# Another bank pair for one query product, the output gate read by ScalarE, and thin products spread out among wide ones

## The chip, the cores and the metric

One NeuronCore of a Trainium2 chip runs the whole program. The metric is device time in microseconds (us); smaller is better. Engines are named as in the profile: PE (TensorE matmuls), PEld (its weight loads), DVE (VectorE), ACT (ScalarE), POOL (GpSimd), SP (SyncE, which here issues the weight DMAs). PSUM has eight banks of 512 float32 columns, numbered 0 to 7; they matter for this change.

## The reference

Two transformer blocks over 256 tokens of width 1024, in float32. The first block mixes a stick-breaking attention and an RWKV-7 time mix; the second has a dilated attention with a short convolution, a cross attention to a memory, and an MLP. What the change touches:

```
# RWKV-7 branch, first block
g  = sigmoid(xg) @ g_up                              # the output gate
kk = (k * k_k) per head
kk = kk / max(norm(kk, per head), 1e-12)             # 8 heads of 64
...
y  = group_norm(wkv7_scan(...)) * lnx_w + lnx_b
bonus = sum(r * k * r_k, per head) * v
out = (y + bonus) * g

# second block
proj = rms_norm(x) @ w_in_2 ; q, k, v, ... = split(proj)
```

The norm per head needs a sum over the 64 features of each head. Features lie on partitions, so the kernel makes the sum with a product by a 0/1 matrix `gather` that gives 8 rows (one per head), and copies the 8 inverses back to all features by a product with a 0/1 matrix `spread` whose contraction has 8 rows. These are the products of few columns and of few rows.

## The kernel before, in words

Every weight matrix is cut into units of 128x2048 elements (1 MB). SP loads a unit into `raw`; ACT rounds it to `whi` (L1271), DVE takes the rest `wlo = raw - whi` (L1762, called `lo`), and PE multiplies with both. There are three buffers of each, so unit u+3 is rounded when PE has used unit u. All engines run programs of their own, in a fixed order written out by hand, and wait for each other by semaphores. Nothing reorders the work.

Activations are held as `xh` and `xl` (together `xhl`). `by_feature` multiplies one unit with 48 matmuls of 256 columns. `by_feature_wide` does it with 16 matmuls of 512 columns (`whi` against both halves) and 16 of 256 (`wlo`), in two output tiles f = 0 and 1, one per bank of a pair. ACT copies the second halves out of the banks (`second_halves`), and then DVE adds the first halves (`summed`). A bank pair is free again when `summed` has been signalled.

First block, where the change touches it:

- The loop over `U_RW` (7 units, in banks 0, 1, 3). After the fifth unit (i = 4) PE makes the four `gather` products (two instructions each) into bank 4. ACT takes the square root after it has seen the end of the sixth unit (i = 5, `krs`), and DVE in its own step i = 5 clamps it and takes the reciprocal (L1850, L1851), which signals `kk_rs`. After that DVE changes the keys (L1855, L1856) and goes on with step 6.
- The loop over `U_QK` (4 wide units, bank pairs (6,7) and (0,1) in turn). After the first one PE waits for `kk_rs` and makes the four `spread` products into banks 4 and 5. Before the second one it waits for `out_evac` 7, DVE's read of the last `U_RW` unit (L1823).
- The value units `U_V` (two). Between them PE makes the gate product into banks 4 and 5 (`gup`) and the bonus product into banks 6 and 7 (`rkk`), and signals `bonus_mm`. DVE then reads the gate twice: times `lnx_w` into `rw[:, 0:4]` (L1897), and, after the bonus (L1899), as the factor of `rw[:, 4:8]` (L1903), which signals `gn_pre`.
- PE waits for `gn_pre` before it overwrites banks 4 and 5 with the first attention logits (`sk`, `sq`), and then runs eight gate units.

Second block, at its start: `keys_around("n3", U_KM[1])` multiplies a unit of the memory keys into banks 0 and 1 and turns the rows of x in banks 2 to 5. Then come the four query and key units `U_QK2`: the first by `by_feature` into bank 6, followed by a small product that copies the norm's row (`dg`, `one`) into bank 4, the second (wide) into banks 0 and 1, the third into 6 and 7, the fourth into 0 and 1. Because banks 0 and 1 still hold the memory keys, the second waits for `summed` of `km`, which DVE makes in `key_sum(1)` behind a `lo`.

Of the kernel before, what the change touches and what calls it, by code (L numbers as in the profile page):

```python
# [6 lines left out]
P = 128  # L7
SEQ = 256
# [4 lines left out]
NPAIR = HW // P  # L13
HD = 64
NH = HW // HD
# [71 lines left out]
def block_kernel(nc, A, out, dbg=None):  # L87
# [9 lines left out]
    with ctx:  # L97
# [5 lines left out]
        def sem(name):  # L103
            if name not in sems:
                sems[name] = ctx.enter_context(nc.semaphore(name))
            return sems[name]
# [142 lines left out]
        def bank(b):  # L249
            return PS[:, b * 512:(b + 1) * 512]  # L250
# [4 lines left out]
        def halved(kind, n):  # L255
            return sum(HALVED[o] for o in list(HALVED)[:list(HALVED).index(kind)]) + n
# [6 lines left out]
        def C(name):  # L263
            a, b = CCOL[name]
            return cst[:, a:b]
# [5 lines left out]
        def par_col(name, i=0):  # L271
            c = PCOL[name] + i
            return par[:, c:c + 1]
# [76 lines left out]
        VM_BANKS = (0, 1, 4, 5)  # L350
        MLP_BANKS = ((2, 3), (0, 1))
        QK_BANKS = ((6, 7), (0, 1))
        QK2_BANKS = (None, (0, 1), (6, 7), (0, 1))
        KM_BANKS = (0, 1)
        RW_BANK = [(0, 1, 3)[i % 3] for i in range(len(U_RW))]

# [84 lines left out]
        def _(pe):  # L441
            def mm(o, l, r, start, stop, **kw):
                return nc.tensor.matmul(o, l, r, start=start, stop=stop, **kw)  # L443
# [75 lines left out]
            def by_feature_wide(u, both, banks, later=0, before=None, between=None, amidst=None, first=None):  # L519


                n = units[u][1]
                wh, wl = split(u, n, later)
                for f in range(2):
                    if before:
                        before(f)
                    fs = slice(f * P, (f + 1) * P)
                    o = bank(banks[f])
                    for k in range(KD):
                        if amidst:  # L530
                            amidst(f, k)
                        mm(o, wh[:, k, fs], both[:, k].rearrange("p a t -> p (a t)"), k == 0, False, skip_group_check=True)
                    for k in range(KD):
                        last = mm(o[:, 0:SEQ], wl[:, k, fs], both[:, k, 0], False, k == KD - 1, skip_group_check=True)
                    if f == 0:
                        if first:
                            last.then_inc(sem(first), 1)
                        if between:
                            between()
                last.then_inc(sem("units_used"), 1)  # L540

            def by_token(u, hi, lo, k0, b, first, end, later=0, between=None):

                n = units[u][1]
                kt = UNIT // n
                wh, wl = split(u, n, later)
                nc_ = n // 512
                if end:
                    steps = [(k, t, c) for t in range(NT) for c in range(nc_) for k in range(kt)]
                else:  # L550
                    steps = [(k, t, c) for k in range(kt) for t in range(NT) for c in range(nc_)]
                for k, t, c in steps:
                    ts = slice(t * P, (t + 1) * P)
                    o = bank(b[t * nc_ + c] if isinstance(b, tuple) else b + t * nc_ + c)
                    ns = slice(c * 512, (c + 1) * 512)
                    mm(o, hi[:, k0 + k, ts], wh[:, k, ns], first and k == 0, False)
                    mm(o, hi[:, k0 + k, ts], wl[:, k, ns], False, False)
                    last = mm(o, lo[:, k0 + k, ts], wh[:, k, ns], False, end and k == kt - 1)
                    if end and k == kt - 1 and (t, c) != (NT - 1, nc_ - 1):
                        last.then_inc(sem("part_done"), 1)  # L560
                        if between:
                            between(t, c)
                last.then_inc(sem("units_used"), 1)
# [88 lines left out]
            def amid_first(i):  # L652
                if i == 0:
                    return lambda part: first_rows(1) if part == 1 else None
                if i == 2:
                    return lambda f: scale_row("n1", 2)
                if i == 3:
                    return lambda f: lora_products()

            for i, u in enumerate(U_RW):  # L660
                if i >= 3:
                    pe.wait_ge(sem("out_evac"), i - 2)
                by_feature(u, xh, xl, RW_BANK[i], None if i else "n1", amid_first(i))
                if i == 4:

                    pe.wait_ge(sem("kk_sq"), 1)
                    pe.wait_ge(sem("lora_evac"), 1)
                    pe.wait_ge(sem("cst_loaded"), 16)
                    for j in range(NPAIR):
                        last = mm(PS[0:NH, 4 * 512:4 * 512 + SEQ], C("gather")[:, NH * j:NH * (j + 1)], kq[:, j, :], j == 0,  # L670
                                  j == NPAIR - 1)
                    last.then_inc(sem("kk_ss"), 1)

            for i, u in enumerate(U_QK):
                if i == 1:
                    pe.wait_ge(sem("out_evac"), 7)
                elif i >= 2:
                    pe.wait_ge(sem("summed"), halved("qk", i - 1))
                by_feature_wide(u, xhl, QK_BANKS[i % 2])
                if i == 0:  # L680

                    pe.wait_ge(sem("kk_rs"), 1)
                    for j in range(NPAIR):
                        last = mm(PS[:, 4 * 512 + j * SEQ:4 * 512 + (j + 1) * SEQ], C("spread")[0:NH, j * P:(j + 1) * P], krs[:],
                                  True, True)
                    last.then_inc(sem("kk_spread"), 1)
            for i, u in enumerate(U_V):
                by_token(u, xh, xl, 4 * i, 2, i == 0, i == 1)
                if i == 0:
# [159 lines left out]
                    pairs(kk, eP, "pair_mm", 4)  # L849

            pe.wait_ge(sem("gn_pre"), 1)
            def gate_unit(i):

                before(i)
                if i == 0:
                    pe.wait_ge(sem("summed"), halved("qk", 4))
                else:
                    pe.wait_ge(sem("summed"), halved("gate", i))
                by_feature_wide(U_G[i], xhl, (0, 1), between=lambda: amid(i))
                behind(i)  # L860
# [206 lines left out]
            for i, u in enumerate(U_QK2):  # L1067
                if i == 0:
                    by_feature(u, xh, xl, 6, "n3")
                    scale_row("n3", 4)  # L1070
                    continue
                if i == 1:
                    pe.wait_ge(sem("summed"), halved("km", 2))
                elif i == 2:
                    pe.wait_ge(sem("out2_evac"), 1)
                else:
                    pe.wait_ge(sem("summed"), halved("qk2", 1))
                by_feature_wide(u, xhl, QK2_BANKS[i])
            by_token(U_V2[0], xh, xl, 0, 2, True, False)

            def dilated_logits(p_):
# [185 lines left out]
        def _(act):  # L1267
# [14 lines left out]
            def hi(u, n=0, step=0):  # L1282

                if u >= NU:
                    return
                act.wait_ge(raw_loaded[u % RING], 16 * (u // RING + 1) + 16 * (step // RING) * n)
                if u >= RING:
                    act.wait_ge(sem("units_used"), u - RING + 1 + step * n)
                A_(whi[u % RING][:], raw[u % RING][:], ACT.Copy).then_inc(sem("hi_done"), 1)

            def after(u):

                hi(u + RING)
                act.wait_ge(sem("units_used"), u + 1)
# [100 lines left out]
            for i, u in enumerate(U_QK):  # L1395
                act.wait_ge(sem("units_used"), u + 1)
                second_halves((sq, sk)[i // 2][:, 2 * (i % 2):2 * (i % 2) + 2, :], QK_BANKS[i % 2]).then_inc(sem("second"), 1)
                hi(u + RING)
            hi(U_V[0] + RING)
            after(U_V[1])  # L1400
            act.wait_ge(norm_sem("n1", "dg"), nth("n1", "dg", 1))
            for t in range(NT):
# [344 lines left out]
        def _(dve):  # L1747
# [144 lines left out]
            lo(U_V[0] + RING)  # L1892

            dve.wait_ge(sem("bonus_mm"), 1)
            dve.wait_ge(sem("rw_pre"), 1)
            for j in range(NPAIR):
                V.tensor_scalar(rw[:, j, :], PS[:, 4 * 512 + j * SEQ:4 * 512 + (j + 1) * SEQ], par_col("lnx_w", j), None, ALU.mult)  # L1897
            for j in range(2):
                last = V.tensor_tensor(bon[:, 2 * j:2 * j + 2, :], bank(6 + j).rearrange("p (j t) -> p j t", j=2),  # L1899
                                       rw[:, 8 + 2 * j:10 + 2 * j, :], ALU.mult)  # L1900
            link(last)
            for j in range(NPAIR):
                last = V.scalar_tensor_tensor(out=rw[:, 4 + j, :], in0=bon[:, j, :], scalar=par_col("lnx_b", j),  # L1903
                                              in1=PS[:, 4 * 512 + j * SEQ:4 * 512 + (j + 1) * SEQ], op0=ALU.add, op1=ALU.mult)
            last.then_inc(sem("gn_pre"), 1)
            lo(U_V[1] + RING)
            def pair_out(dst, mask, n_, b=2):

# [510 lines left out]
```

## Time and profile before

| | |
|---|---|
| median of 3 runs | 841.4 us (840.96 to 841.78) |
| profiled execution | 841.16 us, of which the profile's span is 839.4 us |
| PE busy | 824.6 us, 98% |
| DVE busy | 586.9 us, 70% |
| ACT busy | 430.8 us, 51% |
| mean granted clock of TensorE | 0.997 of full speed |

The span is cut by the profile into what each engine did; 1.8 us of the execution's time lie outside it. The time of a row is the start in us from the start of the span, then the duration; an idle time in square brackets is what lay ahead of it on that engine, and who ended it.

### The profile page before, as it was taken

To read this page: it belongs to the slowest core of one execution; us is meant where nothing else is said; L and a number is where in the kernel's file an instruction comes from. 1 tells how busy PE (TensorE), PEld (TensorE's weight loads), DVE (VectorE), ACT (ScalarE), POOL (GpSimd) and SP (SyncE) were. 2 spreads that over 40 slices of the span, in tenths; PEclk is the share of its full clock that TensorE was granted. 3 is DMA by queue.
4 is the path that set the end of the run, shared out by engine and by line. 5 is a ranking of instruction groups with operands and counts; after the bars stand their busy time and mean duration, and the time that the engine had idled before them with its cause. 6 is when DMAs were issued, how large, how long until landed. Compare 5 with 4: busy or idle time off the path is not lost.

```text
span 839.4 us, 14921 instructions
## 1 busy us (share of the span) xinstructions
PE 824.6 (98%) x6332; PEld 715.2 (85%) x6332; DVE 586.9 (70%) x693; ACT 430.8 (51%) x529; POOL 6.4 (1%) x8
## 2 busy tenths in 40 slices
PE   9999999999999999999998999999999999999997
PEld 9998788888989888888887888888888888888885
DVE  5999865656887666656678567795764866676664
ACT  6644344474387544544466365546654544444443
POOL 0000010000000000000000000000000000000000
PEclk9999999999999999999999999999999999999999
DMA  9845513331764555565545553546423365555541
GB/s 301 289 152 177 175 53 102 103 102 52 280 209 159 180 201 185 165 216 185 200 157 177 168 194 108 192 143 201 167 100 126 133 228 182 180 180 183 192 149 50
DMA packets 96999, 140.55 MB, mean 167 GB/s; under 512 B 2480, under 2 KB 79408, under 8 KB 96944
## 3 DMA queue, kind: packets, MB, share of 16 engines
q1 hardware_dynamic: 96512, 139.36, 49.7%
q8 instruction: 43, 0.70, 0.3%
q10 hardware_dynamic: 432, 0.39, 0.2%
q14 instruction: 12, 0.10, 0.0%
HBM read 138.69 MB, written 1.05 MB: 166 GB/s over the span
## 4 chain that ended last, share of the span: by engine, by line
PE 83%; DVE 10%; ACT 3%; issue 3%; DMA 1%; POOL 0%; ACTq 0%; DVEq 0%; POOLq 0%
PE PS L443 81%; DVE wlo L1762 3%; ACT whi L1271 1%; PE PS L569 1%; DMA raw<-in_w_in_dram 1%; ACT st L1271 1%; DVE rw L1828 1%; ACT xhl L1271 1%; DVE diff L1825 1%; DVE stg L1823 1%; PE PS L1100 0%; DVE cs L1845 0%; PE PS L716 0%; DVE xhl L1789 0%; DVE TT L1924 0%
## 5 line engine op out<-in xcount | busy, mean ns | idle before, releaser
L1762 DVE TENSOR_TENSOR wlo<-raw,whi 128x2048 fp32r<-128x2048 f32 x122 | 278.2, 2289 | 78.7 <-ACT whi L1271 78.5
L443 PE MATMUL PS<-xhl,whi 128*128 128x512 f32 (+1 forms) x1328 | 308.5, 365 | 3.9 <-DVE km L1767 2.9
L1271 ACT ACTIVATE whi<-raw 128x2048 fp32r<-128x2048 f32 (+1 forms) x130 | 241.3, 1859 | 93.6 <-PE PS L443 90.1
L443 PEld LDWEIGHTS PS<-xhl,whi 128*128 128x128 f32 x1328 | 230.3, 190 | 40.3 <-DVE km L1767 3.1
L443 PE MATMUL PS<-xhl,wlo 128*128 128x256 f32 x1136 | 180.3, 282 | 0.1
L443 PEld LDWEIGHTS PS<-xhl,wlo 128*128 128x128 f32 x1136 | 163.7, 191 | 9.7 <-DVE wlo L1803 0.3
L443 PE MATMUL PS<-whi,fh 128*128 128x512 f32 x216 | 84.3, 391 | 0.0
L443 PE MATMUL PS<-wlo,fh 128*128 128x512 f32 x216 | 84.3, 390 | 0.0
L443 PE MATMUL PS<-whi,fl 128*128 128x512 f32 x216 | 84.0, 389 | 0.0
L1767 DVE TENSOR_TENSOR fa<-PS,fa 128x512 f32<-128x512 f32 x25 | 17.3, 691 | 62.7 <-ACT fa L1271 62.7
L443 PEld LDWEIGHTS PS<-whi,fl 128*128 128x128 f32 x216 | 40.6, 188 | 8.6
L443 PEld LDWEIGHTS PS<-whi,fh 128*128 128x128 f32 x216 | 40.7, 188 | 7.8
L443 PEld LDWEIGHTS PS<-wlo,fh 128*128 128x128 f32 x216 | 40.7, 188 | 7.5
L1271 ACT ACTIVATE fa<-PS 128x512 f32<-128x512 f32 x25 | 14.7, 589 | 52.4 <-PE PS L443 52.4
L1789 DVE SCALAR_TENSOR_TENSOR xhl<-PS,par,xhl 128x256 fp32r<-128x256 f32 x40 | 16.7, 476 | 11.7 <-ACT xhl L1271 11.7
L1271 ACT ACTIVATE fh<-fa 128x512 fp32r<-128x512 f32 x16 | 10.1, 633 | 25.9 <-DVE fa L2357 25.9
L1271 ACT ACTIVATE xhl<-PS,par 128x256 fp32r<-128x256 f32 x40 | 15.7, 481 | 12.1 <-PE PS L569 12.1
L443 PE MATMUL PS<-whi,memhl 128*128 128x512 f32 x64 | 20.7, 397 | 0.1
L443 PE MATMUL PS<-whi,xhl 128*128 128x512 f32 x64 | 20.7, 394 | 0.0
L1271 ACT ACTIVATE fh<-fb 128x512 fp32r<-128x512 f32 x11 | 7.0, 632 | 24.9 <-DVE fb L2173 24.9
L1271 ACT ACTIVATE gates<-PS 128x512 f32<-128x512 f32 x8 | 4.8, 597 | 27.9 <-PE PS L443 27.9
L1271 ACT ACTIVATE junk<-xres 128x1024 f32<-128x1024 f32 (+1 forms) x14 | 13.2, 945 | 9.9 <-DVE xres L2116 8.7
(327 smaller groups left out, 1035.3 us busy)
## 6 DMA issues: line engine op xcount, KB each, us to landing
raw<-in_w_in_dram SPq DMA_DIRECT2D x32, 1024.0 KB, 5.3
raw<-in_w_up_dram SPq DMA_DIRECT2D x16, 1024.0 KB, 5.3
raw<-in_w_down_dram SPq DMA_DIRECT2D x16, 1024.0 KB, 5.1
raw<-in_w_ffn_gate_dram SPq DMA_DIRECT2D x11, 1024.0 KB, 5.3
raw<-in_w_ffn_up_dram SPq DMA_DIRECT2D x11, 1024.0 KB, 5.3
raw<-in_w_ffn_down_dram SPq DMA_DIRECT2D x11, 1024.0 KB, 5.6
raw<-in_w_kv_mem_dram SPq DMA_DIRECT2D x8, 1024.0 KB, 5.3
raw<-in_w_o_dram SPq DMA_DIRECT2D x4, 1024.0 KB, 8.2
```

The costliest lines, as they stand in the source:

```text
L443: return nc.tensor.matmul(o, l, r, start=start, stop=stop, **kw)
L569: last = nc.tensor.transpose(PS[:, o:o + P], src[:, t, f * P:(f + 1) * P], C("ident"))
L1271: return nc.scalar.activation(o, i, f, **kw)
L1762: V.tensor_tensor(wlo[u % RING][:], raw[u % RING][:], whi[u % RING][:].bitcast(f32), ALU.subtract) \
L1767: return V.tensor_tensor(dst, tiles(banks)[:, :, 0], dst, ALU.add)
L1789: V.scalar_tensor_tensor(out=lo_[:, f0 + f, :], in0=PS[:, b * 512 + c * SEQ:b * 512 + (c + 1) * SEQ], scalar=par_col(g, f), in1=hi_[:, f0 ...
L1823: V.tensor_tensor(s[:, :, 1:SEQ + 1], two(RW_BANK[i]), spread(rs1[:]), ALU.mult).then_inc(sem("out_evac"), 1)
L1825: link(V.tensor_tensor(diff[:], s[:, :, 0:SEQ], s[:, :, 1:SEQ + 1], ALU.subtract))
L1828: last = V.scalar_tensor_tensor(out=rw[:, r, :], in0=diff[:, f, :], scalar=par_col("mu_rw", r), in1=s[:, f, 1:SEQ + 1], op0=ALU.mult, op1= ...
```

## The change

Three edits, each with its semaphores:

1. The second query unit of the second block goes to banks 2 and 3 instead of 0 and 1. The wait for `summed` of `km` moves to the fourth unit, which still uses banks 0 and 1. The first value unit, which uses banks 2 and 3, gets a wait for the second unit's sum.
2. ACT reads the output gate from PSUM: times `lnx_w` into `rw[:, 0:4]`, and as it is into `rw[:, 4:8]`, then signals `g_read`. DVE reads only the bonus from PSUM, signals `gn_pre` right behind that, and makes the last product out of SBUF. PE waits for both.
3. The four `gather` products no longer stand in one row after the fifth unit: they stand in the sixth unit's first tile, ahead of k = 0, 2, 4 and 6. The four `spread` products no longer stand after the first wide unit: they stand inside it, ahead of k = 2 and k = 6 of each of its two tiles. The wait for `kk_rs` goes with the first of them.

```diff
-        QK2_BANKS = (None, (0, 1), (6, 7), (0, 1))
+        QK2_BANKS = (None, (2, 3), (6, 7), (0, 1))
@@ PE
+            def gather_squares(f, k):
+                if f or k % 2:
+                    return
+                j = k // 2
+                if j == 0:
+                    pe.wait_ge(sem("kk_sq"), 1)
+                    pe.wait_ge(sem("lora_evac"), 1)
+                    pe.wait_ge(sem("cst_loaded"), 16)
+                last = mm(PS[0:NH, 4 * 512:4 * 512 + SEQ], C("gather")[:, NH * j:NH * (j + 1)], kq[:, j, :], j == 0, j == NPAIR - 1)
+                if j == NPAIR - 1:
+                    last.then_inc(sem("kk_ss"), 1)
+            def spread_norms(f, k):
+                if k not in (2, 6):
+                    return
+                j = 2 * f + k // 4
+                if j == 0:
+                    pe.wait_ge(sem("kk_rs"), 1)
+                last = mm(PS[:, 4 * 512 + j * SEQ:4 * 512 + (j + 1) * SEQ], C("spread")[0:NH, j * P:(j + 1) * P], krs[:], True, True)
+                if j == NPAIR - 1:
+                    last.then_inc(sem("kk_spread"), 1)
             for i, u in enumerate(U_RW):
                 ...
-                by_feature(u, xh, xl, RW_BANK[i], None if i else "n1", amid_first(i))
-                if i == 4:
-                    (the four gather products, with the same waits)
+                by_feature(u, xh, xl, RW_BANK[i], None if i else "n1", amid_first(i), 0, gather_squares if i == 5 else None)
             for i, u in enumerate(U_QK):
                 ...
-                by_feature_wide(u, xhl, QK_BANKS[i % 2])
-                if i == 0:
-                    pe.wait_ge(sem("kk_rs"), 1)
-                    (the four spread products)
+                by_feature_wide(u, xhl, QK_BANKS[i % 2], amidst=None if i else spread_norms)
...
             pe.wait_ge(sem("gn_pre"), 1)
+            pe.wait_ge(sem("g_read"), 1)
...
-                if i == 1:
+                if i == 2:
+                    pe.wait_ge(sem("out2_evac"), 1)
+                elif i == 3:
                     pe.wait_ge(sem("summed"), halved("km", 2))
-                elif i == 2:
-                    pe.wait_ge(sem("out2_evac"), 1)
-                else:
-                    pe.wait_ge(sem("summed"), halved("qk2", 1))
                 by_feature_wide(u, xhl, QK2_BANKS[i])
+            pe.wait_ge(sem("summed"), halved("qk2", 1))
             by_token(U_V2[0], xh, xl, 0, 2, True, False)
@@ ACT, between hi(U_V[0] + RING) and after(U_V[1])
+            act.wait_ge(sem("bonus_mm"), 1)
+            act.wait_ge(sem("rw_pre"), 1)
+            for j in range(NPAIR):
+                A_(rw[:, j, :], PS[:, 4 * 512 + j * SEQ:4 * 512 + (j + 1) * SEQ], ACT.Copy, scale=par_col("lnx_w", j))
+            for j in range(2):
+                last = A_(rw[:, 4 + 2 * j:6 + 2 * j, :], bank(4 + j).rearrange("p (j t) -> p j t", j=2), ACT.Copy)
+            last.then_inc(sem("g_read"), 1)
@@ DVE
-            dve.wait_ge(sem("rw_pre"), 1)
-            for j in range(NPAIR):
-                V.tensor_scalar(rw[:, j, :], PS[...], par_col("lnx_w", j), None, ALU.mult)
             for j in range(2):
                 last = V.tensor_tensor(bon[...], bank(6 + j)..., rw[...], ALU.mult)
-            link(last)
+            last.then_inc(sem("gn_pre"), 1)
+            dve.wait_ge(sem("gn_pre"), 1)
+            dve.wait_ge(sem("g_read"), 1)
             for j in range(NPAIR):
-                last = V.scalar_tensor_tensor(out=rw[:, 4 + j, :], ..., in1=PS[...], op0=ALU.add, op1=ALU.mult)
-            last.then_inc(sem("gn_pre"), 1)
+                last = V.scalar_tensor_tensor(out=rw[:, 4 + j, :], ..., in1=rw[:, 4 + j, :], op0=ALU.add, op1=ALU.mult)
+            link(last)
```

## Rows read from the trace of the kernel before

**Rows 1.** Page, part 1: engine, busy us, share of span, instructions.
```profile
PE 824.6 (98%) x6332; PEld 715.2 (85%) x6332; DVE 586.9 (70%) x693; ACT 430.8 (51%) x529; POOL 6.4 (1%) x8
```

**Rows 2.** Waits of PE: released by, total us, times, longest us.
```profile
PE PS L443 <- DVE km L1767: 2.9, 1, 2.9
PE PS L443 <- DVE rw L1903: 1.8, 1, 1.8
```

**Rows 3.** Stretches: length; busy us of PE, PEld, DVE, ACT, POOL; PEclk; DMA.
```profile
30.00:60.00 30.00, 30.00 (x223) 27.38 (x220) 29.38 (x44) 13.53 (x15) 0.00 (x0) 1.00 0.66 217
60.00:94.50 34.50, 32.54 (x165) 27.18 (x163) 34.07 (x40) 16.03 (x13) 0.00 (x0) 1.00 0.56 176
```

**Rows 4.** PE in order of time at the start of the second block.
```profile
455.09 0.71 PE L443 MATMUL PS<-dg,one 128*128 128x128 f32 x4
458.74 3.63 PE L443 MATMUL PS<-xhl,whi 128*128 128x512 f32 x8 [2.94 <-DVE km L1767]
462.21 1.11 PE L443 MATMUL PS<-xhl,wlo 128*128 128x256 f32 x8
```

**Rows 5.** The same view as group 3, of two stretches there.
```profile
455.60:458.70 3.10, 0.20 (x2) 0.01 (x1) 2.90 (x3) 2.35 (x3) 0.00 (x0) 0.99 0.95 322
458.70:462.10 3.40, 3.36 (x8) 2.69 (x9) 2.78 (x2) 0.00 (x0) 0.00 (x0) 0.51 0.85 263
```

**Rows 6.** DVE in order of time, same place.
```profile
452.15 2.29 DVE L1762 TENSOR_TENSOR wlo<-raw,whi 128x2048 fp32r<-128x2048 f32 x1 [0.76 <-ACT whi L1271]
...
455.80 2.29 DVE L1762 TENSOR_TENSOR wlo<-raw,whi 128x2048 fp32r<-128x2048 f32 x1 [0.76 <-ACT whi L1271]
458.01 0.68 DVE L1767 TENSOR_TENSOR km<-PS,km 128x512 f32<-128x512 f32 x1
458.61 0.68 DVE L2199 TENSOR_TENSOR q<-PS,rs 128x512 f32<-128x512 f32 x1
```

**Rows 7.** PE in order of time around the gather products.
```profile
39.56 0.28 PE L443 MATMUL PS<-xhl,wlo 128*128 128x256 f32 x1
39.77 1.89 PE L443 MATMUL PS<-kq,cst 128*8 128x256 f32 x8
...
41.93 0.28 PE L443 MATMUL PS<-xhl,wlo 128*128 128x256 f32 x1
```

**Rows 8.** PE in order of time, first two wide units and the spread products.
```profile
53.21 2.00 PE L443 MATMUL PS<-xhl,whi 128*128 128x512 f32 x8
...
57.84 1.11 PE L443 MATMUL PS<-xhl,wlo 128*128 128x256 f32 x8
58.89 1.99 PE L443 MATMUL PS<-krs,cst 8*128 8x256 f32 x8
60.91 2.11 PE L443 MATMUL PS<-xhl,whi 128*128 128x512 f32 x8
62.87 1.11 PE L443 MATMUL PS<-xhl,wlo 128*128 128x256 f32 x8
...
66.94 0.50 PE L443 MATMUL PS<-xhl,whi 128*128 128x512 f32 x1 [0.17 <-DVE sq L1767]
```

**Rows 9.** DVE in order of time, steps 5 and 6 of its loop.
```profile
55.72 1.74 DVE L1851 RECIPROCAL krs<-krs 8x256 f32<-8x256 f32 x1
...
60.18 0.68 DVE L1823 TENSOR_TENSOR stg<-PS,rs 128x512 f32<-128x512 f32 x1
```

**Rows 10.** PE in order of time, end of the value units.
```profile
92.36 0.39 PE L443 MATMUL PS<-whi,xhl 128*128 128x512 f32 x1
94.50 0.92 PE L443 MATMUL PS<-sq,sk 64*128 64x256 f32 x8 [1.75 <-DVE rw L1903]
```

**Rows 11.** DVE in order of time, same place.
```profile
91.48 1.28 DVE L1899 TENSOR_TENSOR bon<-PS,rw 128x512 f32<-128x512 f32 x2
92.79 1.66 DVE L1903 SCALAR_TENSOR_TENSOR rw<-bon,par,PS 128x256 f32<-128x256 f32 x4
```

**Rows 12.** ACT in order of time: four reads of PSUM with a bias, and a wait.
```profile
36.02 1.55 ACT L1271 ACTIVATE sg<-PS,par 128x256 f32<-128x256 f32 x4
...
92.85 1.91 ACT L1271 ACTIVATE whi<-raw 128x2048 fp32r<-128x2048 f32 x1 [7.00 <-PE PS L443]
```

More of the change, by code:

```diff
@@ L662, in _ @@
                     pe.wait_ge(sem("out_evac"), i - 2)
-                by_feature(u, xh, xl, RW_BANK[i], None if i else "n1", amid_first(i))
-                if i == 4:
-                    pe.wait_ge(sem("kk_sq"), 1)
-                    pe.wait_ge(sem("lora_evac"), 1)
-                    pe.wait_ge(sem("cst_loaded"), 16)
-                    for j in range(NPAIR):
-                        last = mm(PS[0:NH, 4 * 512:4 * 512 + SEQ], C("gather")[:, NH * j:NH * (j + 1)], kq[:, j, :], j == 0,
-                                  j == NPAIR - 1)
-                    last.then_inc(sem("kk_ss"), 1)
+                by_feature(u, xh, xl, RW_BANK[i], None if i else "n1", amid_first(i), 0, gather_squares if i == 5 else None)
             for i, u in enumerate(U_QK):
@@ L678, in _ @@
                     pe.wait_ge(sem("summed"), halved("qk", i - 1))
-                by_feature_wide(u, xhl, QK_BANKS[i % 2])
-                if i == 0:
-                    pe.wait_ge(sem("kk_rs"), 1)
[L683 to L686, printed above, removed]
+                by_feature_wide(u, xhl, QK_BANKS[i % 2], amidst=None if i else spread_norms)
             for i, u in enumerate(U_V):
@@ L1894, in _ @@
             dve.wait_ge(sem("bonus_mm"), 1)
-            dve.wait_ge(sem("rw_pre"), 1)
-            for j in range(NPAIR):
-                V.tensor_scalar(rw[:, j, :], PS[:, 4 * 512 + j * SEQ:4 * 512 + (j + 1) * SEQ], par_col("lnx_w", j), None, ALU.mult)
             for j in range(2):
@@ L1900, in _ @@
                                        rw[:, 8 + 2 * j:10 + 2 * j, :], ALU.mult)
-            link(last)
+            last.then_inc(sem("gn_pre"), 1)
+            dve.wait_ge(sem("gn_pre"), 1)
+            dve.wait_ge(sem("g_read"), 1)
             for j in range(NPAIR):
                 last = V.scalar_tensor_tensor(out=rw[:, 4 + j, :], in0=bon[:, j, :], scalar=par_col("lnx_b", j),
-                                              in1=PS[:, 4 * 512 + j * SEQ:4 * 512 + (j + 1) * SEQ], op0=ALU.add, op1=ALU.mult)
-            last.then_inc(sem("gn_pre"), 1)
+                                              in1=rw[:, 4 + j, :], op0=ALU.add, op1=ALU.mult)
+            link(last)
             lo(U_V[1] + RING)
```

## The prediction

> **What bounds the kernel now.** I read the page's busy shares first: PE is busy for 98% of the span [rows 1], so only its pauses and its clock can give anything back. The table of waits of PE names two pauses worth having, 2.9 us ended by DVE's sum of the memory keys and 1.8 us ended by DVE's last use of the gate [rows 2]. Each is one that the change takes away. Third I read the busy time by stretch. From 30 to 94.5 us DVE is nearly as full as PE: 29.38 of 30 us, then 34.07 of 34.5 us [rows 3]. There DVE runs late behind PE, and a wait of PE for DVE that the change puts earlier has to be priced against DVE's own clock time. Last I read both engines in order of time at each place, and the granted clock around the long pause.
>
> **Edit 1, other banks (second block).** After the small row product at 455.09 us, whose four matmuls start 0.11 apart and whose stream is thus done at about 455.64, PE stands still until 458.74 [rows 4]. It waits for the memory-key sum, which DVE starts at 458.01, behind a 2.29 us `lo` [rows 6]. The second unit needs nothing else: its own `lo` is the one of 452.15 to 454.44 [rows 6], and banks 2 and 3 were last read for the operands that the first unit has already multiplied. So it starts at 455.64: 3.10 us earlier, and 0.11 more because a product that follows a wait starts slower (its first eight matmuls take 2.11 against 2.00 us, [rows 8]). The pause has a second price. In the stretch behind it the granted clock is 0.51 of full speed, 1.2 instead of 2.4 GHz, and back at 1.00 after that; during the pause PE did nothing [rows 5]. The eight wide matmuls took 458.74 to 462.21, 3.47 us, where the same eight after a wait take 60.91 to 62.87, 1.96 us [rows 8]: 1.51 us. With no pause there is no reason for the clock to fall. Sum: 3.10 + 0.11 + 1.51 = 4.72 us gained.
>
> Is something late next? The third unit would start at 455.64 + 5.58 = 461.2 (a wide unit is 53.21 to 57.84 plus eight matmuls of 0.12, [rows 8]). It needs the `lo` that ends at 458.09 and the first unit's read that ends at 459.29 [rows 6]. Both are done 2 us before. The fourth needs the key sum (458.69), the value unit a sum that DVE makes about 1.3 us after the second unit ends; both have a unit or two of room. From there on ACT and DVE work behind PE at the pace of its units, as before, and the gain is kept to the end. Bounds: 3.0 us if the clock falls here all the same, 4.8 at best.
>
> **Edit 2, ACT takes the gate.** PE's last value product starts at 92.36 and would let the logits start at 92.68 (0.23 for its stream, 0.09 to change to 64 rows); they start at 94.50 [rows 10], 1.82 us later. DVE did 4 multiplies by `lnx_w`, the bonus (1.28) and then 1.66 us of final products before `gn_pre` [rows 11]. Now `gn_pre` comes behind the bonus. ACT's reads: four of 128x256 take 1.55 us by the nearest row, and two of twice the width not more than 1.55 together [rows 12], so at most 3.1 us, in a hole of 7.00 us in which ACT waits for the end of the value units [rows 12]. Nothing but its own next `hi` is queued behind them. DVE's final products wait for `g_read` and so hold up the `lo` behind them, but that one waits for the `hi` after the value units anyway. Alone, this edit is worth the 1.82 us. Whether it still is depends on when PE comes here, which edit 3 decides.
>
> **Edit 3, the thin products.** First their direct price. The gather row: from the dense matmul at 39.56 to the one at 41.93 is 2.37 us, of which three dense steps are 0.36 and the eight instructions at 0.216 each 1.73 [rows 7]; 0.28 us is left for going to 8 columns and back. Four excursions instead of one: 3 x 0.28 = 0.85 us more on PE. The spread row: the dense work of the first wide unit ends at 58.79 and the next unit starts at 60.91, effectively 61.02 with its slower start; of these 2.23 us 1.73 are the products, 0.10 is the wait for L1823 (60.18 + 0.68, [rows 8, 9]), and 0.40 is the way in and out. Four excursions cost 4 x 0.40.
>
> The Trainium skill speaks against this edit. Its page TensorEngine Tiling (Array Packing), section Key Properties, says that changing the tiling mode drains the TensorE. If each thin product counts as such a change, eight excursions pay it where two did. The 0.28 and 0.40 us above are this case's numbers for it, and they are in the sum.
>
> Then the wait. The spread products need the reciprocal that DVE ends at 57.46 [rows 9]. Before, PE asked for it at 58.79, after the whole unit. Now it asks at k = 2 of the first tile. The unit starts at 53.21 + 0.85 = 54.06, two wide matmuls take 0.46, so PE is at the wait at 54.52 and stands there until about 57.50: **a new pause of 3.0 us**. Nothing makes DVE earlier: it is full up to that point [rows 3], its order is unchanged up to there, and the square root that it needs comes from ACT after the sixth unit, one unit before it is due. This pause hides the 0.85 us of the gather.
>
> From 57.50: the rest of the unit 5.58 - 0.46 = 5.12 us, the spread products 1.73, their excursions 1.60 less the 0.10 of the first way in, which the wait hides. The unit ends at 65.85. In the old kernel this point is 61.02, so PE is 4.83 us late. It wins back what it used to wait before the third unit: from 60.91 to 66.94 is 6.03 us for a unit of 5.58, 0.45 us [rows 8]. That leaves 4.38 us. From here PE is the later of the two engines: DVE's first query sum came at 66.21 and will come within half a us of that, and its queue has until 92.6 + 4.4 = 97.0 us for what it had done at 94.45. PE thus reaches the logits at 92.68 + 4.38 = 97.06 instead of 94.50: **2.56 us lost**. The gate is ready then even by the old order, give or take 0.1, so edit 2's 1.82 us are swallowed by edit 3 and not to be added.
>
> **Sum.** -4.72 + 2.56 = -2.16 us. Against the profiled execution's 841.16 us that is 839.0; this execution lies 0.24 below the median of 841.4, so I say 839.3 us. Below, 0.2% (1.7 us) is what a measurement of this kernel can tell from no change.
>
> **What isn't priced yet: the clock at the new pause.** A pause of 3.1 us halved the clock [rows 4, 5]; the one of 1.8 us did not, the clock is 1.00 over its stretch [rows 3]. The new one, 3.0 us, is nearer to the first. Bounds: 0, and 1.5 us if the loss of the old place comes again. That one case is too little to know whether 3.0 us always do it, and before and after this pause PE is at work; I give it somewhat less than even.
>
> **The rivals.**
> - *Clock halved at the new pause* (B). For: the row of the second block. It moves the 1.51 us from there to here: 839.3 + 1.5 = 840.8 us. The change then is within what can't be told from none.
> - *Clock halved, and kept low by the thin products* (C), the slower case. Behind the old pause PE ran dense 512-column products, and the clock was back after 3.4 us. Behind the new one a third of the time goes to products of 8 rows. If these don't count as work and the clock stays at half until the unit ends, the 8.3 us from 57.5 cost 1.51/1.96 = 77% more, 6.4 us: 845.7. It decides the sign from about 2.2 us on, that is if the clock stays low much longer than the 3.4 us of the old place. Against: between 30 and 60 us eight thin instructions in one row left the clock at 1.00 [rows 3, 7].
> - *No new pause* (D): the wait is met because DVE gets through earlier than its rows say. Then edit 3 costs PE 0.85 + 1.20 - 0.45 = 1.6 us, edit 2 gives back its 1.82, and the sum is -4.9: 836.5. Against: DVE has 0.6 us of idle time in the 30 us before 60, so it can't be 3 us earlier.
> - *Edit 1 doesn't do what it says* (E): the second unit starts early but the third waits in its place. Then the 4.72 shrink towards zero and edit 3's 2.56 stand alone: 844. Against: the 2 us of room above.
>
> **Chances.** Forecast (A) 0.48, own range 838.4 to 840.2; B 0.32 (840.2 to 841.6); C 0.07; D 0.06; E 0.03; the rest, 0.04, is spread. Leaving out C, most of D and E gives a range of 837.6 to 842.2. Faster by over 0.2% means under 839.7: nearly nine tenths of A, all of D and a little of B, 0.51. Slower by over 0.2% means over 843.1: C and E in the main, 0.08. Within: 0.41.
>
> **What would show it.** In the order of time, PE with an idle time of about 3 us ended by DVE's `krs` reciprocal, near 57.5, and the first wide unit ending near 65.9; the granted clock of 57 to 62 us tells A from B, and that of 62 to 66 B from C. The logits at about 97, with no wait for `rw`. The `g_read` copies on ACT in a hole of its time. Near 458 (2.6 us later than now) no wait for `km`, and a clock of 1.00. The prediction is wrong if PE meets `kk_rs` without a pause, if an excursion costs clearly more than 0.4 us, or if another unit of the second block takes over the wait.

## The result

The change made the kernel slower: 842.91 us median of 20 runs (840.62 to 847.32) against 841.29 us of the kernel before (20 runs, 839.58 to 842.99), so the medians lie 1.6 us apart; the ratio over all runs is 1.0029 with a 95% interval of 1.0017 to 1.0042. The forecast was 839.3 us, range 837.6 to 842.2. The profiled execution of the changed kernel took 845.2 us, of which 843.4 are the span. The 20 single runs lie in groups: four from 840.6 to 841.3, seven from 842.1 to 843.1, six from 845.1 to 845.4 and three above 846.5. The mean granted clock of the single runs goes down with the groups: 0.995 to 0.997, then 0.993 to 0.994, 0.990 to 0.991, and 0.988. The profile below is from the third group.

The waits of PE after the change (released by, total us, times, longest). They answer to [rows 2]: both old waits are gone, one new one is there.

```profile
PE PS L443 <- DVE krs L1866: 2.7, 1, 2.7
PE PS L443 <- POOL one L1255: 1.0, 1, 1.0
PE PS L443 <- ACT xhl L1279: 0.7, 2, 0.3
```

PE in order of time in the first wide unit. It answers to [rows 8].

```profile
54.24 0.63 PE L443 MATMUL PS<-xhl,whi 128*128 128x512 f32 x2
57.58 0.69 PE L443 MATMUL PS<-krs,cst 8*128 8x256 f32 x2 [2.71 <-DVE krs L1866]
58.20 1.22 PE L443 MATMUL PS<-xhl,whi 128*128 128x512 f32 x4
59.36 1.22 PE L443 MATMUL PS<-krs,cst 8*128 8x256 f32 x2
60.50 1.22 PE L443 MATMUL PS<-xhl,whi 128*128 128x512 f32 x2
61.52 1.91 PE L443 MATMUL PS<-xhl,wlo 128*128 128x256 f32 x8
...
71.24 2.78 PE L443 MATMUL PS<-xhl,whi 128*128 128x512 f32 x8
```

PE asks for the reciprocal after two wide matmuls and gets it at 57.58. From the second thin product on everything takes nearly twice as long: eight `wlo` matmuls take 1.91 us where they took 1.11 [rows 8]. The stretches of the same profile (length; busy us of PE, PEld, DVE, ACT, POOL; granted clock; DMA share; GB/s) say why:

```profile
54.50:57.50 3.00, 0.37 (x2) 0.00 (x0) 2.97 (x4) 2.98 (x2) 0.00 (x0) 1.00 0.24 33
57.50:59.30 1.80, 1.72 (x6) 0.96 (x6) 1.70 (x7) 0.21 (x1) 0.00 (x0) 0.99 1.01 380
59.30:72.90 13.60, 13.60 (x37) 9.38 (x37) 7.70 (x14) 4.37 (x5) 0.00 (x0) 0.50 0.28 97
72.90:78.00 5.10, 5.10 (x31) 4.51 (x30) 4.05 (x3) 1.17 (x2) 0.00 (x0) 1.00 0.11 25
```

The clock is at half (1.2 instead of 2.4 GHz) for 13.6 us, four times as long as in [rows 5], and it does not fall during the pause but 1.8 us after its end. DVE, the full engine here before [rows 3], now works for only 7.70 of 13.60 us: 5.76 us of the rest it waits for ACT's copy of a second half (`sq`, until 72.11), which follows PE's late unit.

PE at the logits, against [rows 10]: no wait, but at 103.25 instead of 94.50.

```profile
102.94 0.39 PE L443 MATMUL PS<-whi,xhl 128*128 128x512 f32 x1
103.25 0.92 PE L443 MATMUL PS<-sq,sk 64*128 64x256 f32 x8
```

ACT in the same stretch, against [rows 12]: it takes the gate in 2.54 us (97.91 to 100.45), in a hole of its time, and is done 2.8 us before PE comes for the banks at 103.25.

```profile
97.91 1.57 ACT L1279 ACTIVATE rw<-PS,par 128x256 f32<-128x256 f32 x4 [1.48 <-PE PS L443]
99.35 1.10 ACT L1279 ACTIVATE rw<-PS 128x512 f32<-128x512 f32 x2
103.42 1.91 ACT L1279 ACTIVATE whi<-raw 128x2048 fp32r<-128x2048 f32 x1 [2.97 <-PE PS L443]
```

PE at the start of the second block, against [rows 4]: the second query unit follows the row product at once, and at full speed (2.09 us for eight wide matmuls instead of 3.63).

```profile
463.87 0.71 PE L443 MATMUL PS<-dg,one 128*128 128x128 f32 x4
464.33 2.09 PE L443 MATMUL PS<-xhl,whi 128*128 128x512 f32 x8
466.27 1.11 PE L443 MATMUL PS<-xhl,wlo 128*128 128x256 f32 x8
```

So the books of this execution are: 8.75 us later at the logits (103.25 - 94.50), 4.7 us won back at 464 us, 4.0 us longer in the span (843.4 - 839.4).

### The profile page after: what moved, and what is told of

It is laid out like the page before. It is cut to its first block, busy times and chain, and to the rows that moved or that the text cites. A ratio compares the mean times of both kernels' runs of the same rounds, so it can differ in the third digit from the quotient of the medians.

```text
span 843.4 us, 14925 instructions
## 1 busy us (share of the span) xinstructions
PE 830.9 (99%) x6332; PEld 717.1 (85%) x6332; DVE 585.8 (69%) x689; ACT 433.4 (51%) x535; POOL 6.4 (1%) x8
## 4 chain that ended last, share of the span: by engine, by line
PE 91%; DVE 5%; ACT 2%; issue 2%; DMA 1%; ACTq 0%
PE PS L443 89%; DVE wlo L1777 1%; PE PS L569 1%; ACT st L1279 1%; DMA xres<-in_x_dram 1%; ACT whi L1279 1%; DVE rw L1843 0%; DVE diff L1840 0%; DVE stg L1838 0%; PE PS L1108 0%; DVE cs L1860 0%; PE PS L724 0%; DVE st L1985 0%; ACT xhl L1279 0%; DVE krs L1866 0%
## 5 line engine op out<-in xcount | busy, mean ns | idle before, releaser
L443 PE MATMUL PS<-xhl,whi 128*128 128x512 f32 (+1 forms) x1328 | 311.7, 366 | 0.8 <-ACT xhl L1279 0.7
```

## Experiments

The theory going in: edit 1 wins 4.7 us and edit 2 up to 1.8; edit 3 loses on PE's path by its pause and its excursions, and loses 1.5 us more for every 3.4 us of halved clock, which thin products behind a pause prolong. Every kernel was timed 5 to 11 times beside the kernel before, on one chip per group (one for `e1_banks` to `e12_banks_gate`, another for `p1_pause_row` to `p3_full_pieces` and `p7_full_rows`, the first again for `p8_thin_no_wait` and `p4_gather_only`). In the first group the kernel before took 841.55 us, in the second 841.57, in the third 841.39. Gains are differences of medians; the ratios are taken over all runs.

**One edit at a time.** `e1_banks` is the kernel before with edit 1:

```diff
-        QK2_BANKS = (None, (0, 1), (6, 7), (0, 1))
+        QK2_BANKS = (None, (2, 3), (6, 7), (0, 1))
   (and the waits of the change's first part)
```

> Edit 1 alone: the second query unit of the second block in banks 2 and 3. Theory: it takes away the 3.1 us pause of PE, its slow restart and the low clock behind it, so 4.7 us: about 836.6 us beside 841.3, with no wait for km in the profile, and the clock at 1.00 from 455 to 470 us. It is tied to nothing in the first block, so it gives the same in full whatever edits 2 and 3 do. Rival 1: the clock falls at some other place instead, then only the pause is won, 3.1 us: 838.2. Rival 2: another wait of the second block takes its place: over 840.

Measured: 836.74 us (836.55 to 837.22), ratio 0.9944 [0.9930, 0.9958]: 4.8 us faster. No wait for `km`; the clock is 1.00 from 455 to 470 us. Both rivals fall. Its profile also shows something that the profile of before did not: behind the unchanged row of spread products the clock is at half.

```profile
58.00:61.30 3.30, 3.30 (x18) 2.60 (x17) 3.16 (x9) 0.86 (x1) 0.00 (x0) 1.00 0.64 247
61.30:64.80 3.50, 3.50 (x11) 2.79 (x10) 3.46 (x5) 3.50 (x5) 0.00 (x0) 0.51 0.03 7
64.80:70.00 5.20, 5.20 (x31) 4.57 (x31) 5.17 (x8) 2.42 (x3) 0.00 (x0) 1.00 0.62 202
```

PE has no pause worth the name there: 3.30 of 3.30 us busy ahead of the fall, 1.99 of them in products of 8 rows. So the clock can fall behind a row of thin products with no pause, in some executions and not in others. In time it cost little here: this execution is the fastest of its five (836.55 us). The wait for `rw` is 0.6 us in it instead of the 1.8 of [rows 2], so 1.2 of the 1.5 us came out of that wait.

`e2_gate` is the kernel before with edit 2 (ACT's six reads, `gn_pre` behind the bonus, PE's wait for `g_read`).

> Edit 2 alone: ACT reads the gate. Theory: PE comes to the logits at 92.7 us instead of 94.5 and the gain is kept: 1.8 us, about 839.5 us. Rival: DVE or ACT is behind PE in the eight gate units anyway, so that PE waits there for what it won: within 0.3 us of the kernel before.

Measured: 840.22 us (839.37 to 841.77), ratio 0.9981 [0.9972, 0.9990]: 1.3 us faster. The wait for `rw` is gone and the gain is kept in the main, so the rival falls; it is 0.5 us short of the 1.8. Its profiled execution was the slowest of its eleven and has the half clock behind the spread row as well (61.4 to 64.8 us), and for 6.8 us at the old place at 457. When the clock falls at 61 us PE comes later to the value units' end and the wait for `rw` is shorter to begin with (0.6 us in `e1_banks`), so there is less to win. Without edit 2 DVE lets PE go on at 94.50 in the kernel before and at 94.59 in `e1_banks`, whenever PE comes. That this is why 0.5 us are missing from the median is likely, not shown.

`e3_thin` is the kernel before with edit 3, both `gather_squares` and `spread_norms`.

> Edit 3 alone: the thin products in pieces. Theory: a pause of 3.0 us at the reciprocal of krs, then the clock at 1.2 GHz for several stretches while thin products are mixed in; logits at 97 us plus 1.5 us for each 3.4 us of low clock. So about 4.7 us above the whole change: 847.6 us, single runs from 845 to 852. Rival: the loss of the whole change comes from edit 1 or 2, and this one is under 1 us slower than before: below 842.3.

Measured: 848.83 us (845.61 to 850.77), ratio 1.0075 [1.0053, 1.0097]: 7.3 us slower, 1.2 more than expected; what the 1.2 are stays open. The whole loss of the change, and more, is edit 3. The low stretch of its profile is the one of the whole change again:

```profile
57.50:59.60 2.10, 1.26 (x5) 0.84 (x6) 2.03 (x6) 0.96 (x1) 0.00 (x0) 1.00 0.91 288
59.60:73.30 13.70, 13.70 (x38) 9.01 (x37) 7.52 (x15) 3.72 (x5) 0.00 (x0) 0.50 0.32 107
```

`e12_banks_gate` is the change without edit 3.

> Edits 1 and 2 without edit 3. Theory: both gains stand beside each other, 4.7 + 1.8 = 6.5 us: about 834.8 us, with hardly any spread between runs, since both long pauses of PE are gone. Rival: edit 2's gain is lost in the gate units: 836.6.

Measured: 835.27 us (834.85 to 836.85), ratio 0.9928 [0.9914, 0.9942]: 6.3 us faster than before. The two gains stand beside each other. It is faster than both kernels. The "hardly any spread" is a miss: one of six runs is at 836.85. In its profile the clock is at 1.00 up to the logits, and PE comes to them without a wait at 93.28, not at 92.68; it was 0.7 us later than in the kernel before already at the spread row (59.56 against 58.89), ahead of anything that edit 2 touches.

**Pause, thin products, or both.** `p1_pause_row` is the whole change, with the pause but without thin products inside the unit:

```diff
             def spread_norms(f, k):
-                if k not in (2, 6):
-                    return
-                (one product)
+                if (f, k) == (0, 2):
+                    pe.wait_ge(sem("kk_rs"), 1)
...
                 by_feature_wide(u, xhl, QK_BANKS[i % 2], amidst=None if i else spread_norms)
+                if i == 0:
+                    (the four spread products in one row)
```

> The whole change, but the first wide unit only waits for kk_rs at k = 2 and has no thin products inside; the four spread products follow it in one row, as before. The 3 us pause stays. Theory (thin products mixed in hold the clock low behind the pause): the clock is low for one stretch of 3.4 us, at most two, and the time is 838.1 us plus 1.5 for each: 839.6 to 841. Rival (the pause alone makes a long low stretch): the clock stays low as long as in the whole change, and the time is its 842.9 less the 1.2 us of three excursions saved: 841.7 or more.

Measured: 839.81 us (838.36 to 840.04), ratio 0.9975 [0.9966, 0.9985]. Two of ten runs are at 838.4, the other eight within 0.5 us of 839.8: the sum without a low stretch, and with one. The profile has the same pause and one short low stretch:

```profile
54.50:57.50 3.00, 0.35 (x2) 0.00 (x0) 2.96 (x4) 2.98 (x2) 0.00 (x0) 1.00 0.23 28
57.50:58.50 1.00, 0.94 (x4) 0.79 (x5) 0.93 (x5) 0.19 (x1) 0.00 (x0) 1.00 0.96 356
58.50:61.90 3.40, 3.40 (x14) 3.01 (x13) 3.26 (x8) 1.49 (x2) 0.00 (x0) 0.50 0.46 179
61.90:66.00 4.10, 4.10 (x22) 3.48 (x22) 4.10 (x7) 2.91 (x4) 0.00 (x0) 1.00 0.05 8
```

So a pause of this length is mostly followed by a lower clock (eight runs of ten), and without the thin pieces behind it for 3.4 us only, by this profile and by the times. The rival, that the pause alone makes the long stretch, falls.

`p2_thin_late` is the whole change with the same four pieces in the second wide unit, where nothing has to be waited for on their account:

```diff
-                by_feature_wide(u, xhl, QK_BANKS[i % 2], amidst=None if i else spread_norms)
+                by_feature_wide(u, xhl, QK_BANKS[i % 2], amidst=spread_norms if i == 1 else None)
```

> The whole change, but the four spread products stand inside the second wide unit instead of the first, where kk_rs has long come: the same thin products among wide ones, no pause. Theory (it needs the pause): the clock stays at 1.00, PE reaches the logits at about 95.5 us, and the time is 837.6 us with little spread. Rival (thin products among wide ones lower the clock by themselves): the clock falls in the sixth RWKV unit or in this one in most runs, 839 to 843 us.

Measured: 838.48 us (837.56 to 840.61), ratio 0.9958 [0.9944, 0.9971]. Two of five runs are at the 837.6 of the theory, two near 838.5, and one, the profiled one, 3 us above. That one has the clock at half for 6.8 us from 62.5 us on, over three of the four pieces, behind the 1.0 us wait for `stg`:

```profile
62.50:69.30 6.80, 6.80 (x19) 4.46 (x19) 6.77 (x9) 3.16 (x3) 0.00 (x0) 0.50 0.48 156
```

The theory's "little spread" is a miss: with thin pieces and without the 3 us pause the clock can be low too, but no run of the five has the length of the change.

`p8_thin_no_wait` puts the four pieces closer together, in that unit's second tile, 3 us behind the wait:

```diff
-                if k not in (2, 6):
+                if f == 0 or k % 2:
                     return
-                j = 2 * f + k // 4
+                j = k // 2
```

> As p2_thin_late, but the four spread products all stand in the second tile of the second wide unit, ahead of k = 0, 2, 4 and 6, so that no wait lies near them: 2.8 us of wide products before, and thin and wide ones in close turns, 2.1 us of wide whi products to 3.3 us of thin ones and their excursions. The low stretches of p2 began at 62.5 us, behind a 1.0 us wait and the first piece. Theory (thin products count as too little work, whatever the wait): this closer mixture lowers the clock in most runs, 839 to 842 us. Rival (it takes a pause before them): the clock stays at 1.00 and all runs are near 837.6 us.

Measured: 838.23 us (837.65 to 839.54), ratio 0.9959 [0.9946, 0.9973]: between the two. PE in order of time, from its profile (839.22 us):

```profile
64.09 0.69 PE L443 MATMUL PS<-krs,cst 8*128 8x256 f32 x2
64.72 0.73 PE L443 MATMUL PS<-xhl,whi 128*128 128x512 f32 x2
65.38 0.69 PE L443 MATMUL PS<-krs,cst 8*128 8x256 f32 x2
...
67.95 0.69 PE L443 MATMUL PS<-krs,cst 8*128 8x256 f32 x2
68.58 1.12 PE L443 MATMUL PS<-xhl,whi 128*128 128x512 f32 x2
69.50 1.91 PE L443 MATMUL PS<-xhl,wlo 128*128 128x256 f32 x8
```

The first rows give the price of an excursion at full clock: a thin piece and two wide matmuls take 65.38 - 64.09 = 1.29 us, of which 0.46 is the wide ones and 0.43 the piece's stream, so 0.40 us, the figure of the prediction. The last rows take nearly twice their time: the clock falls right after the last piece, with PE busy throughout since its wait for `stg` ended at 61.10, and stays low for 3.4 us.

```profile
65.30:68.70 3.40, 3.40 (x12) 1.60 (x12) 3.37 (x6) 0.47 (x1) 0.00 (x0) 1.00 0.76 240
68.70:72.10 3.40, 3.40 (x13) 3.02 (x14) 2.43 (x2) 0.66 (x2) 0.00 (x0) 0.50 0.45 117
72.10:75.50 3.40, 3.40 (x20) 2.97 (x19) 3.01 (x3) 1.74 (x1) 0.00 (x0) 1.00 0.75 260
```

The fastest two runs, at 837.65 and 837.88, have no room for that. A pause right ahead of the fall is not needed, then (the 1.3 us wait for `stg` ended 7.6 us ahead of it); but by their times these five runs hold about one short stretch at most, so the theory's "most runs, 839 to 842" is a miss, and nothing here comes near 13.6 us.

`p3_full_pieces` is the whole change, pause and places unchanged, with each piece made full:

```diff
-        krs = at("krs", W + 94, [NH, SEQ])
+        krs = at("krs", W + 94, [P, SEQ])
-mm(PS[0:NH, 4 * 512:4 * 512 + SEQ], C("gather")[:, NH * j:NH * (j + 1)], kq[:, j, :], ...)
+mm(PS[:, 4 * 512:4 * 512 + SEQ], cst[:, CCOL["gather"][0] + NH * j:CCOL["gather"][0] + NH * j + P], kq[:, j, :], ...)
-mm(PS[...], C("spread")[0:NH, j * P:(j + 1) * P], krs[:], True, True)
+mm(PS[...], C("spread")[:, j * P:(j + 1) * P], krs[:], True, True)
   (and ACT's square root reads all 128 rows)
```

> The whole change with its pause and its eight pieces at their places, but each piece made with 128 rows and 128 columns: the gather product takes the 128 constant columns that begin with its eight (the other 120 sums are not used), the spread product contracts over 128 rows, of which 120 have weight zero. Same result, same streamed columns, same float32. Theory (few rows and columns are what holds the clock low, and what makes the excursion cost): at most one low stretch, no excursions: 837.5 us, 839 with one stretch. Rival (the pause, or float32 products in between, hold it low): as the whole change, near 842.9, low for over 10 us in the profile.

Measured: 839.75 us (839.22 to 840.77), ratio 0.9979 [0.9970, 0.9988], 3.2 us less than the change, with nothing moved. By the expectation 1.8 of these are excursions saved (839.3 to 837.5), so about 1.4 are left for the clock. The profiled execution, the slowest of eleven:

```profile
53.50:57.00 3.50, 0.12 (x1) 0.00 (x0) 3.47 (x3) 2.95 (x2) 0.00 (x0) 1.00 0.09 14
57.00:57.70 0.70, 0.00 (x0) 0.00 (x0) 0.70 (x2) 0.00 (x0) 0.00 (x0) 0.50 0.74 123
57.00:63.80 6.80, 6.05 (x18) 5.12 (x19) 6.59 (x14) 2.96 (x3) 0.00 (x0) 0.50 0.43 147
63.80:67.00 3.20, 3.20 (x18) 2.75 (x17) 2.72 (x5) 0.00 (x0) 0.00 (x0) 1.00 0.26 45
```

The low stretch is 6.8 us, half of the change's, although PE now stands still longer (4.12 us instead of 2.71 by the profile, since it saves the gather's excursions and comes earlier). Its first 0.75 us lie still in the pause, which ends at 57.75: here the clock fell before PE went on, unlike in the change. So this is no pure comparison of widths, but a longer pause should, if anything, make its low stretch longer, and none of its eleven runs is above 840.8, where nine of the change's twenty are above 845. I had expected one stretch at most. The rival, that pause or float32 alone hold the clock down as long as in the change, falls. PE in order of time, same profile, at full clock again, shows that a full piece is no excursion: a piece and four wide matmuls (0.93) take 65.69 - 64.33 = 1.36 us, which leaves 0.43, the bare stream of the piece.

```profile
64.33 0.59 PE L443 MATMUL PS<-krs,cst 128*128 128x256 f32 x2
64.58 1.27 PE L443 MATMUL PS<-xhl,whi 128*128 128x512 f32 x4
65.69 0.59 PE L443 MATMUL PS<-krs,cst 128*128 128x256 f32 x2
```

**The better version, and the gather.** `p7_full_rows` is `e12_banks_gate` with both rows of products made full as above. `p4_gather_only` is `e12_banks_gate` with `gather_squares` alone.

> Edits 1 and 2 without edit 3, and the gather and spread products, in one row each as before, made with 128 rows and 128 columns as in p3_full_pieces. Theory: the occasional low stretch behind the thin rows goes, and the 0.28 and 0.3 us of their excursions: 834.4 us against 835.3 of edits 1 and 2, with all runs within 0.6 us. Rival (the width of a product doesn't matter to the clock): 834.6 or more, with single runs 1.5 us above the rest.

Measured: 835.08 us (834.83 to 835.30), ratio 0.9923 [0.9909, 0.9936]. All five runs lie within 0.5 us, where those of `e12_banks_gate` spread over 2.0. The median is 0.2 us lower, 0.7 less than expected: what the excursions give back is met by the wait for `stg` (0.4 us, 61.02 us). The median is on the rival's side (834.6 or more), the spread on the theory's; but `e12_banks_gate` has one run of six that stands out, so five runs without one don't show that wide rows keep the clock up. It has the lowest median of this study, 7.8 us below the change's, though from `e12_banks_gate` it can't be told.

> Edits 1 and 2 and of edit 3 the gather pieces alone; the spread products stay in one row behind the first wide unit. Theory: the pieces cost PE 0.85 us directly, of which the waits at the second and third wide units hide about 0.45: 835.7 us against 835.3 for edits 1 and 2, and the clock at 1.00 around them (39 to 48 us). Rival 1: they lower the clock as the spread pieces do: 837 us or more. Rival 2: all hidden: 835.3.

Measured: 835.37 us (835.18 to 837.01), ratio 0.9930 [0.9917, 0.9944]. With 0.1 us over `e12_banks_gate`, rival 2 (hidden) is nearer than the theory's 0.4, and the difference is too small to tell. Its profile is on the theory's side: from the first wide unit to the gate product PE takes 29.93 us (54.34 to 84.27) where `e12_banks_gate` takes 30.40 (53.88 to 84.28), so the waits on the way hid 0.47 us, about the 0.45 expected, and not all 0.85. The clock is 1.00 in its profile from 38 to 80 us: it fell at the gather pieces (8 columns in the stationary operand, all 128 rows) in none of the profiles here.

## Why the prediction was wrong

Step by step, by the prediction's own terms:

- *Edit 1, 4.72 us.* Right in size and in kind: 4.8 us alone, and 4.7 in the profile of the change. No later wait took its place. Two small slips cancel: the next unit can start 0.46 us after the row product (463.87 to 464.33), not 0.55, so the pause was 3.19 us and not 3.10; and the slow start stays, since the eight matmuls behind the row product take 1.94 us where eight with no wait or small product ahead take 1.84 (53.21 to 55.05 in the kernel before).
- *Edit 2, 1.82 us, swallowed by edit 3.* Right in kind, and less than 1.82 in time: alone 1.3 us, beside edit 1 1.5 us (836.74 to 835.27). The 1.82 hold only if PE comes at 92.68; in `e12_banks_gate` it comes at 93.28, 1.2 us ahead of the old 94.50. With edit 3 PE came to the logits without a wait and late. ACT's 2.54 us for the gate were inside the bound of 3.1.
- *Edit 3, the pause.* Right: PE at the wait at 54.70 (54.24 + 0.46), released at 57.58 (forecast 54.52 and 57.50), so 2.9 us instead of 3.0. The excursions were 0.28 and 0.40 us as forecast. Its direct price, 2.56 us, fits the runs: with no low stretch the sum is 839.3, with one 840.8, and the fastest runs of the change are at 840.6 to 840.8. `p1_pause_row` (838.4 and 839.8) and `p2_thin_late` (837.6) meet the same sum with their own terms.
- *The clock behind the pause.* This is the step that failed: I took "no fall" as the likeliest, 0.48, because I gave the halved clock "somewhat less than even". In 20 runs of the change none is near 839.3. And I held it unlikely (rival C, 0.07) that the thin products would keep it down, on the ground that eight thin instructions in one row had left the clock at 1.00 between 30 and 60 us. That ground was the wrong product: [rows 7] is the gather row, 128 rows by 8 columns, while the pieces behind the pause are spread products, of 8 rows. The gather pieces left the clock at 1.00 in every profile here. The spread row of the kernel before ends at about 60.9 and left it at 1.00 in that one execution, but `e1_banks` and `e2_gate` show the same row followed by a halved clock. The row given for the 1.8 us pause, [rows 3] from 60 to 94.5, couldn't tell either, because it ends with the pause; the trace has 1.00 from 94.5 to 98 us too, so the reading itself holds. In the change the low stretch lasted 13.6 us and cost 6.2 us at the logits (103.25 against the forecast 97.06), close to the 6.4 us that rival C named. None of the three signs that I had listed as proving me wrong came up; none of them was the clock. `p1_pause_row` takes the thin pieces away and is left with one low stretch; `p3_full_pieces` only makes them full and is left with 6.8 us in its slowest run and 839.75 us in the median.

The median of the change, 842.91, is 3.6 us above the sum without a low clock. It lies between one low stretch (840.8) and four (845.2), near two (842.3); the steps of the mean granted clock from group to group fit a low time that varies from run to run, though only one run of the change has a profile. That the long low stretch comes from the pause together with the thin products is shown by taking either away. The medians lie below the change's by 3.1 us (`p1_pause_row`), 4.4 (`p2_thin_late`) and 3.2 (`p3_full_pieces`), but 1.2, 1.7 and 1.8 of these are direct prices by the sums, for excursions and for the pause itself, which leaves 1.9, 2.7 and 1.4 us for the clock. The slowest runs say it more plainly: 840.0, 840.6 and 840.8 us, where nine of the change's twenty lie between 845.1 and 847.3, far more than those direct prices above them. What stays open is how the chip weighs a product of 8 rows against idle time, whether it is the rows or something that goes with them, and why the same kernel meets the low clock in one execution and not in the next.

## What to carry to other kernels

A wait moved into the middle of a unit is priced against the engine that ends it, not against the place it came from: here a product that was ready in time at the unit's end came 3 us too early inside it. Behind a pause, products with few rows went here with a halved clock of 13.6 us instead of 3.4, so they belong away from one. Giving them all 128 rows and columns costs no more streamed columns and takes away the excursion of 0.40 us; whether it also keeps the clock up where there is no pause, five runs within 0.5 us suggest and don't show. And where times of one kernel come in groups (here 1.5 to 3 us apart), look at the granted clock in several profiles before one row is taken as proof that a place is harmless, and look that the row shows the same kind of product.

## What the runs showed of the hardware

- The clock doesn't fall at a fixed place of the pause: 1.8 us after its end in the change (59.3 against 57.58), 1.3 in `e3_thin` (59.6 against 58.34), 1.0 in `p1_pause_row`, and 0.75 us ahead of its end in `p3_full_pieces` (57.0 against 57.75).
- Half clock costs this kernel a little under half its length: 1.5 us for 3.4 us of it in [rows 4, 5], 6.2 us for 13.6 us in the change. Where PE waits later anyway, less of it is lost: `e1_banks` waits 0.6 us for `rw` instead of 1.8.
- Eight products of 8 rows in a row (1.99 us), with PE busy before and after, were followed by 3.5 us at 0.51 in `e1_banks` and 3.4 us at 0.50 in `e2_gate`, and by none in the profiles of the kernel before, `e12_banks_gate` and `p4_gather_only`.
- A product of 8 rows among wide ones takes 0.83 us, one of 128 rows and the same 256 float32 columns 0.43: more rows are cheaper. The Trainium skill's page TensorEngine Tiling (Array Packing), section Key Properties, says that changing the tiling mode drains the TensorE. The 0.40 us fit that, but no run here shows that a product of 8 rows is such a change of mode.
